# GpSimd casts the high weights of each dense unit in four pieces of 256 columns instead of one of 1024

## The reference

```
h = rmsnorm(x);  z = h @ w_in;  gates = sigmoid(h @ w_gate + b)
y = gated sum of (gmlp(z) @ proj_a, pool(z) @ proj_b, diff_attention(z) @ proj_c)
x = x + y @ w_out
x = x + conv_ffn(rmsnorm(x))              # w_up, 3-tap conv, gelu, w_down
x = rmsnorm(x)                            # second block follows
x = x + latent_attention(x, ctx) @ mla_w_out
x = x + fourier_mix(x)                    # fno_w_in, DFTs, fno_w_out
out = rmsnorm(x)
```

## Time and profile before

| | us |
|---|---|
| median of 3 runs | 2516.39 |
| lowest, highest | 2515.13, 2519.18 |
| the profiled execution, its own time | 2517.72 |
| its span, first to last instruction | 2515.8 |
| TensorE busy | 2462.1 (98%) |
| GpSimd busy | 970.8 (39%) |
| VectorE busy | 1446.7 (58%) |
| mean granted TensorE clock | 0.996 |

### The profile page before, as it was taken

The page is one execution under the profiler, slowest core; times in us unless marked ns, Lnnn a source line. Parts: engine busy times, 40 slices in busy tenths (PEclk is TensorE's granted clock), DMA queues, the critical chain, the costliest instruction groups (busy, mean ns, idle before and its releaser), DMA issues.

```text
span 2515.8 us, 33954 instructions
## 1 busy us (share of the span) xinstructions
PE 2462.1 (98%) x12160; PEld 2034.1 (81%) x12160; DVE 1446.7 (58%) x1986; ACT 873.1 (35%) x1293; POOL 970.8 (39%) x1022
## 2 busy tenths in 40 slices
PE   7999999999999999999999999999999999999998
PEld 5777787787787788888888878788998888788886
DVE  6847474735457877777421472277777773633344
ACT  4332222223224554544100142156666661322121
POOL 4334344333444777677444533201000005223242
PEclk9999999999999999999999999999999999999999
DMA  4124343421423223323644211100000002111112
GB/s 176 42 93 151 102 158 108 143 92 42 175 93 126 101 100 117 116 100 111 240 178 164 84 53 34 50 10 9 17 8 8 9 9 69 34 34 33 42 42 75
DMA packets 54419, 210.73 MB, mean 84 GB/s; under 512 B 6420, under 2 KB 7700, under 8 KB 49082
## 3 DMA queue, kind: packets, MB, share of 16 engines
q1 hardware_dynamic: 50340, 194.92, 22.6%
q10 hardware_dynamic: 3990, 14.59, 1.6%
HBM read 173.30 MB, written 38.55 MB: 84 GB/s over the span
## 4 chain that ended last, share of the span: by engine, by line
PE 89%; DVE 4%; issue 2%; ACT 2%; POOL 1%; DMA 1%; DVEq 0%; SPq 0%; ACTq 0%; POOLq 0%
PE PS L749 41%; PE PS L1065 16%; PE PS L1094 9%; PE PS L1348 5%; PE PS L1282 4%; PE PS L1322 3%; PE PS L1288 3%; PE PS L924 1%; PE PS L959 1%; PE PS L1272 1%; PE PS L778 1%; PE PS L1527 1%; PE PS L950 1%; PE PS L1169 1%; PE PS L1511 1%
## 5 line engine op out<-in xcount | busy, mean ns | idle before, releaser
L749 PE MATMUL PS<-H,w_hl 128*128 128x512 f32 x4368 | 1031.2, 394 | 18.7 <-POOL w_hl L675 8.1
L749 PEld LDWEIGHTS PS<-H,w_hl 128*128 128x128 f32 x4368 | 815.4, 189 | 210.5 <-issue 28.2
L694 POOL CAST w_hl<-w_raw 128x1024 fp32r<-128x1024 f32 x138 | 155.3, 1126 | 1360.3 <-PE PS L749 823.1
L675 POOL TENSOR_TENSOR w_hl<-w_raw,w_hl 128x256 fp32r<-128x256 f32 x568 | 511.2, 931 | 11.4
L1065 PE MATMUL PS<-BT,WS 128*128 128x512 f32 x1056 | 247.2, 389 | 1.9 <-DVEq L2707 0.9
L1094 PE MATMUL PS<-FFD,w_hl 128*128 128x512 f32 x1056 | 239.8, 389 | 0.1
L1065 PEld LDWEIGHTS PS<-BT,WS 128*128 128x128 f32 x1056 | 198.0, 188 | 44.5 <-POOL WS L703 2.0
L1094 PEld LDWEIGHTS PS<-FFD,w_hl 128*128 128x128 f32 x1056 | 198.1, 188 | 41.6 <-DVEq L2565 0.5
L703 POOL TENSOR_TENSOR WS<-w_raw,WS 128x256 fp32r<-128x256 f32 x176 | 181.9, 1058 | 47.5 <-ACT WS L1832 46.6
L1065 PE MATMUL PS<-B,WS 128*128 128x512 f32 x792 | 187.0, 389 | 2.4 <-ACT KEEP L1865 2.4
L1065 PEld LDWEIGHTS PS<-B,WS 128*128 128x128 f32 x792 | 148.5, 188 | 33.6 <-POOL WS L703 2.8
(11 more groups left out here) (348 smaller groups left out, 2997.9 us busy)
## 6 DMA issues: line engine op xcount, KB each, us to landing
w_raw<-in_units SPq DMA_DIRECT2D x186, 512.0 KB, 3.7
AW<-in_ada SPq DMA_DIRECT2D x48, 512.0 KB, 4.3
ff_part<-FFS SPq DMA_DIRECT2D x20, 1024.0 KB, 4.9
FFD<-ff_part SPq DMA_DIRECT2D x20, 1024.0 KB, 5.8
X<-in_x SPq DMA_DIRECT2D x8, 512.0 KB, 8.8
x_part<-SC SPq DMA_DIRECT2D x8, 512.0 KB, 2.6
X<-x_part SPq DMA_DIRECT2D x4, 1024.0 KB, 8.6
out<-X SPq DMA_DIRECT2D x16, 256.0 KB, 2.2
```

Of the source, the lines that this page charges most:

```text
L675: ins = pool.tensor_tensor(lo_part[:, part], raw[:, part], hi_part[:, part].bitcast(F32), ALU.subtract)
L694: pool.tensor_copy(hi_part, raw).then_inc(w_hi, 1)
L749: mm = pe.matmul(PS[:, out_at + a:out_at + a + m], w(s, wp, w0 + k), src[:, o:o + m], start=(k == 0 and wp == 0 and xp == 0), stop=(k == k ...
```

## The change

A helper `high_pieces` casts 256 columns at a time, four times, and raises `w_hi` once, with the last. It stands in for the one cast at all three places. What is waited for, and the order of everything else, stay as they are.

```diff
+        def high_pieces(hi_part, raw):
+
+            for a in range(0, UW, 2 * P):
+                ins = pool.tensor_copy(hi_part[:, a:a + 2 * P], raw[:, a:a + 2 * P])
+            ins.then_inc(w_hi, 1)
+
         for s in range(2):
             hi_part, lo_part, raw = split_unit(s, s)
-            pool.tensor_copy(hi_part, raw).then_inc(w_hi, 1)
+            high_pieces(hi_part, raw)
             pool.wait_ge(w_hi, s + 1)
             low_pieces(lo_part, raw, hi_part)
...
                     pool.sem_inc(w_seen, 1)
-                    pool.tensor_copy(hi_part, raw).then_inc(w_hi, 1)
+                    high_pieces(hi_part, raw)
                     pool.wait_ge(w_hi, 2 * i + (s + 1 + his))
...
             hi_part, lo_part, raw = split_unit(s, down0 + s)
-            pool.tensor_copy(hi_part, raw).then_inc(w_hi, 1)
+            high_pieces(hi_part, raw)
             pool.wait_ge(w_hi, down0 + more + s + 1)
```

## The result

The changed kernel takes 2524.21 us (median of 14 runs, 2522.09 to 2525.96), the kernel before 2515.85 us in runs beside it (14 runs, 2512.99 to 2519.18). The ratio is 1.0032, 95% interval 1.0024 to 1.0040: 8.4 us slower, where 2.9 had been forecast and a change of less than 0.2% was held the likeliest. The time lies 0.7 us above the range.

A forecast was written before the change was run, and what follows sets the result against it. TensorE, busy 98% of the span, bounds the kernel, GpSimd being early nearly everywhere. The terms 4.2 - 0.5 - 1.0 - 0.6 + 0.8 give +2.9 us, 2519.3 on the median; range 2515.3 to 2523.5.

The forecast's parts named there:

- a change of less than 0.2%: Whole kernel: the measured time would lie within 0.2%, about 5 us, of the kernel before; chance 0.76.
- A cast piece, 0.36 and 1.45 for four: GpSimd's cast of 256 columns takes 0.36 us alone, 1.45 for a unit, 0.4 more than before.
- the dear piece: Rival: a cast piece costs as much as a subtraction, 0.70 us; sum +12.4, 2529 us; chance 0.22.
- Turns at the start, +4.2: First two units: each cast piece waits out a DVE instruction, 1.31 us a turn; 4.2 us lost in all.
- the pieces do give way: Against the rival that queued casts keep going while DVE waits: +1.6, 2518.0 us; that rival's chance 0.14.
- 0.4, 0.7 and 3.1: Start: first unit's cast 0.4 us longer, its first subtraction behind DVE 0.7, second unit's cast turns 3.1.
- The step that left the lower stretch of the clock unchanged: Start: the lower clock's 2.7 us cost over 15 matmuls stays, with 2 us to both sides for the range.
- The gains, -2.1: DVE freed from whole casts gains 0.5 us at 59, 1.0 at 230 and 0.6 at 2077 us.
- the forecast's own subtraction: At 2077 us: 1.59 less 0.4 less some 0.5 for first matmul and signal leaves 0.6 to 0.7 us.
- The direct waits, two with 0.8: TensorE's waits for GpSimd at L1198 and at 2433 us each grow by 0.4: loss 0.8 us.
- The slack of 2.2 us: Smallest idle time before a cast in steady loops, late in the down projection; a shorter added length costs nothing there.
- Now worse, now better. I put these at nothing: Elsewhere, pieces beginning 0.4 us later meet DVE at another point: counted as zero, with 1 us to both sides.

The follow-up runs named there:

- fixed-order pair: VectorE's first instruction held until the first unit's cast has ended, in the kernel before and in the changed kernel: 2514.27 and 2523.72 us.
- run 4: Kernel before with the first two units' subtraction as one instruction of 1024 columns in place of four: 2508.46 us, ratio 0.9972.

## Why the prediction was wrong

Most of the miss lies in the loops, where the forecast had a gain of 1.3 us and the runs show a loss of 3.1. Two steps of the forecast failed there; the start and the price of a piece came out nearly right.

**A cast piece, 0.36 and 1.45 for four: right.** 0.40 for one (1.43 for four, 1.97 for eight of 128). Each instruction more costs (1.43 - 1.04) / 3 = 0.13 us, so the dear piece did not happen. The Trainium skill (GPSIMD Engine Reference, Performance pitfalls for Q7 kernels) has a cost for each read command, from which 0.26 us for three more was estimated; the runs show 0.39. By direction that rule holds here; that it is the read commands that cost is not shown.

**Turns at the start, +4.2: right as a mechanism, near in size.** The turns (1.34 forecast as 1.31), the first subtraction behind VectorE's first instruction, and TensorE at 26.77 (26.5 forecast) are all in the profile: the pieces do give way. What the forecast had at 0.4, 0.7 and 3.1 measured 0.39, 1.01 and 3.37, so 4.8. Alone, the start costs 5.6 us by medians and 5.0 in the fixed-order pair, of which 0.4 is the load that landed later. The step that left the lower stretch of the clock unchanged held in the first two profiles (15 matmuls each) and not in the fixed-order pair (9 and 14); it varies in kernels of either kind.

**The gains, -2.1: nearly right in sum.** At 59 us 0.26 to 0.33 for a forecast 0.5, at 236 us 0.8 for 1.0, at 2077 us 0.3 for 0.6. The instruction that took 2.06 takes 1.42 now, and the one-column instruction that took 0.80 behind a whole cast takes 0.16:

```profile
64.07 1.42 DVE L2261 TENSOR_TENSOR H<-SC,H 128x1024 fp32r<-128x1024 f32 x1
```

```profile
236.31 0.16 DVE L2419 TENSOR_TENSOR cols<-cols 128x1 f32<-128x1 f32 x1
```

At 2077 TensorE runs into the next wait for a split (0.61 us at 2088), so the gain is what the forecast's own subtraction left, and smaller.

**The direct waits, two with 0.8: the first step that failed.** There are five with 1.8, beside the gain at 2077 that a sixth cuts. The two named were those that the waits of before print; the other three were already at their edge there: the split ended some 0.15 us (2146 and 2482 us of before) and 0.25 us (2164) before TensorE opened the unit. TensorE's weight loads stood still with no releaser shown, since the split ended just in time. At 2482 us in before and at 2487 in after:

```profile
2478.36 3.81 POOL L675 TENSOR_TENSOR w_hl<-w_raw,w_hl 128x256 fp32r<-128x256 f32 x4
2482.29 2.84 PEld L749 LDWEIGHTS PS<-H,w_hl 128*128 128x128 f32 x13 [0.46 <-issue]
```

```profile
2482.83 3.81 POOL L675 TENSOR_TENSOR w_hl<-w_raw,w_hl 128x256 fp32r<-128x256 f32 x4
2486.75 3.29 PEld L755 LDWEIGHTS PS<-H,w_hl 128*128 128x128 f32 x15 [0.85 <-issue]
2486.78 3.45 PE L755 MATMUL PS<-H,w_hl 128*128 128x512 f32 x14 [0.45 <-POOL w_hl L675]
```

The last subtraction ended at 2482.17 and the loads began at 2482.29: no slack, though no wait is printed. The slack of 2.2 us held where it was read: idle before the casts in the down projection's loop is 1.8 to 1.9 now, and TensorE doesn't wait there until there are eight pieces. The cast of the earlier trace rows, after:

```profile
1451.38 1.44 POOL L681 CAST w_hl<-w_raw 128x256 fp32r<-128x256 f32 x4 [1.80 <-PE PS L1100]
```

**"Now worse, now better. I put these at nothing": the second step that failed.** Places other than those costed give 2.8 us of loss and 0.6 of gain. Where a loss was followed to its cause, a VectorE instruction on TensorE's path is met by a subtraction that begins 0.4 later. In before, around 590 us, and then in after:

```profile
586.54 0.16 DVE L2413 TENSOR_TENSOR cols<-cols 128x1 f32<-128x1 f32 x1
...
590.19 0.69 DVE L2424 SCALAR_TENSOR_TENSOR GTB<-GTB,PS 128x512 f32<-128x512 f32 x1
```

```profile
589.67 2.80 POOL L675 TENSOR_TENSOR w_hl<-w_raw,w_hl 128x256 fp32r<-128x256 f32 x4
591.32 0.49 DVE L2419 TENSOR_TENSOR cols<-cols 128x1 f32<-128x1 f32 x1
595.35 0.69 DVE L2430 SCALAR_TENSOR_TENSOR GTB<-GTB,PS 128x512 f32<-128x512 f32 x1
596.18 4.10 PE L755 MATMUL PS<-H,w_hl 128*128 128x512 f32 x17 [0.36 <-DVE GTB L2430]
```

The one-column instruction takes 0.49 in place of 0.16, GTB is late by 5.16 where the instruction ahead of it was late by 4.78, and TensorE waits 0.36. That chain ended in before with TensorE just served. The same VectorE chain, in the traces of before and after, does this at four more of the nine places:

| place in the trace of before | VectorE's instruction that is met | it took, and takes | TensorE's lag gained |
|---|---|---|---|
| 224 us | L2413 | 0.18, 0.57 | 0.39 |
| 316 us | L2413 | 0.16, 0.48 | 0.38 |
| 453 us | L2413 | 0.19, 0.55 | 0.37 |
| 632 us | L2403 | 0.21, 0.59 | 0.39 |

At 367, 2171 and 2197 us too an instruction ahead of what TensorE waits for is met and grows (L2414 from 0.75 to 1.20, after L2413 had shrunk by 0.30; L3118 from 0.75 to 1.14; L3152 from 0.41 to 0.94). The place at 814 us was not followed. That the meetings fell out worse at nine places and better at three (664, 1465 and 2416 us) is as the pieces happened to lie; nothing in the forecast's rows spoke for an even sum.

**The sum.** The loops: 1.8 + 2.8 - 2.0 = +2.6 by profile, +3.1 by runs, forecast 0.8 - 2.1 = -1.3. The start: 5.0 to 5.6, forecast 4.2. These are 4.7 to 5.8 of the missing 5.5 us. What the traces show by its cause, without the load and the clock, is 4.8 at the start and 2.6 in the loops, 7.4 of the 8.4 us; the last 1 us is the part that stays open above.

## What to carry to other kernels

The length of an instruction is not its cost where another engine works beside it without a pause: there each instruction waits its turn, so count instructions (about 1.1 us each here), and cut work only where the other engine's wait is the one that ends last. Before an added 0.4 us is called covered, look for the consumers that begin within some tenths of a microsecond of the producer's end; the list of waits need not print those, and each became a wait of most or all of the addition here (0.29 to 0.43 us).

## What was unexpected of the hardware

- One GpSimd subtraction of 1024 columns beside a busy VectorE takes 3.24 us, and the VectorE instructions that it meets take 2.84 and 3.40 (L2283 and L2285 in run 4) in place of 1.2 to 1.75. At the start this was a gain of 6.7 us, in the loops it cost 8.0: the same edit with opposite signs in two stages.
- The granted clock's lower stretch near 830 or 2068 us, at one, at both or at neither, moves a single execution by up to 2.6 us: as much as one term of the sum. A pair of profiles has to be searched for it before their difference is read as the change.
